# A two-layer hybrid attention encoder: the score products of fourteen head pairs stand one step earlier on TensorE

## The reference, cut to what matters

```python
def mixer_swa_sinks(q, k, v, q_g, k_g, sinks, cos, sin):        # group B; A and C differ in bias, mask and weights
    q = apply_rope(rmsnorm(q, q_g), cos, sin)
    k = apply_rope(rmsnorm(k, k_g), cos, sin)
    ...
    scores = jnp.einsum('bnqhgd,bnjhd->bnhgqj', qc, kb).astype(jnp.float32) * (d ** -0.5)
    ...
    p = jax.nn.softmax(jnp.concatenate([scores, sink], axis=-1), axis=-1)[..., :-1]
    out = jnp.einsum('bnhgqj,bnjhd->bnqhgd', p.astype(v.dtype), vb)

def reference(x, norm1_g, w_in, ...):
    for l in range(DEPTH):                                      # 2
        proj = rmsnorm(x, norm1_g[l]) @ w_in[l]                 # 2048 -> 4352
        ...
        mixed = jnp.concatenate([out_a, out_b, out_c], axis=-1)
        x = x + mixed @ w_out[l]
        h2 = rmsnorm(x, norm2_g[l])
        x = x + jnp.square(jax.nn.relu(h2 @ w_up[l])) @ w_down[l]
```

## Time and profile before

| | |
|---|---|
| median of three runs | 2083.15 us |
| the profiled execution | 2083.34 us |
| its span, first to last instruction | 2081.5 us |
| granted TensorE clock, mean | 1.000 |
| PE busy | 2072.1 us |
| DVE busy | 1270.2 us |
| ACT busy | 993.0 us |
| POOL busy | 190.8 us |

### The profile page before, as it was taken

One profiled execution on the slowest core, in us unless ns is written; L12 is line 12 of the kernel. 1 busy time (PEld: TensorE's weight loads), 2 busy tenths in 40 slices (PEclk: granted clock), 3 DMA queues, 4 the chain that ended last, 5 costly groups with the idle time before them and its releaser, 6 DMA issues.

```text
span 2081.5 us, 26423 instructions
## 1 busy us (share of the span) xinstructions
PE 2072.1 (100%) x10585; PEld 1737.3 (83%) x10585; DVE 1270.2 (61%) x1653; ACT 993.0 (48%) x1328; POOL 190.8 (9%) x196
## 2 busy tenths in 40 slices
PE   8999999999999999999999999999999999999999
PEld 7887788888888888888888877888888888888887
DVE  6767556665565556556676775665655655665664
ACT  5557644443443444344455576444434434443443
POOL 5253100000000000001023521000000000000000
PEclk9999999999999999999999999999999999999999
DMA  8567866666666666666656578666666666666663
GB/s 287 168 189 188 208 197 182 185 192 196 187 191 192 192 187 193 193 187 191 188 176 194 167 192 213 183 185 189 192 193 191 190 194 187 188 193 192 191 191 122
DMA packets 207130, 396.49 MB, mean 190 GB/s; under 512 B 13610, under 2 KB 22032, under 8 KB 207008
## 3 DMA queue, kind: packets, MB, share of 16 engines
q1 hardware_dynamic: 202320, 379.39, 61.5%
q0 software_dynamic: 4512, 15.33, 3.9%
q10 hardware_dynamic: 176, 0.09, 0.0%
HBM read 377.95 MB, written 2.12 MB: 183 GB/s over the span
## 4 chain that ended last, share of the span: by engine, by line
PE 99%; DVE 0%; ACT 0%; DMA 0%; issue 0%; SPq 0%; ACTq 0%; DVEq 0%
PE psum L481 40%; PE psum L501 23%; PE psum L485 20%; PE psum L504 12%; PE psum L511 1%; PE psum L572 1%; PE psum L556 1%; PE psum L599 1%; PE psum L559 1%; DVE probs L1016 0%; PE psum L601 0%; DMA x<-in_x_dram 0%; ACT w_hi L676 0%; PE psum L586 0%; PE psum L587 0%; PE psum L585 0%
## 5 line engine op out<-in xcount | busy, mean ns | idle before, releaser
L852 DVE TENSOR_TENSOR w_lo<-raw_ring,w_hi 128x1024 fp32r<-128x1024 f32 (+1 forms) x692 | 847.1, 1226 | 683.6 <-ACT w_hi L676 682.6
L676 ACT CAST w_hi<-raw_ring 128x1024 fp32r<-128x1024 f32 (+1 forms) x720 | 749.6, 1042 | 1002.0 <-PE psum L485 612.1
L501 PE MATMUL psum<-xt,w_hi 128*128 128x512 f32 x2048 | 512.9, 392 | 0.0
L481 PE MATMUL psum<-w_hi,ht_hi 128*128 128x512 f32 x1280 | 502.1, 392 | 0.0
L481 PE MATMUL psum<-w_hi,ht_lo 128*128 128x512 f32 x1280 | 498.6, 390 | 0.0
L501 PEld LDWEIGHTS psum<-xt,w_hi 128*128 128x128 f32 x2048 | 368.8, 189 | 66.3
L485 PE MATMUL psum<-w_lo,ht_hi 128*128 128x512 f32 x1280 | 342.5, 389 | 0.0
L504 PEld LDWEIGHTS psum<-xt,w_lo 128*128 128x128 f32 x2048 | 279.4, 190 | 20.0
L504 PE MATMUL psum<-xt,w_lo 128*128 128x256 f32 x2048 | 285.6, 282 | 0.0
L481 PE MATMUL psum<-w_hi,xt 128*128 128x512 f32 (+1 forms) x1152 | 282.9, 388 | 1.4 <-DVE xt L889 1.4
L481 PEld LDWEIGHTS psum<-w_hi,ht_hi 128*128 128x128 f32 x1280 | 240.4, 188 | 51.7 <-issue 3.0
(11 more groups left out here) (144 smaller groups left out, 987.0 us busy)
## 6 DMA issues: line engine op xcount, KB each, us to landing
raw_ring<-in_w_up_dram SPq DMA_DIRECT2D x256, 512.0 KB, 3.7
raw_ring<-in_w_down_dram SPq DMA_DIRECT2D x256, 512.0 KB, 3.7
raw_ring<-in_w_in_dram SPq DMA_DIRECT2D x128, 512.0 KB, 4.4
raw_ring<-in_w_out_dram SPq DMA_DIRECT2D x64, 512.0 KB, 4.5
w_lo<-raw_ring POOLq DMA_DIRECT2D x28, 512.0 KB, 5.6
raw_ring<-in_w_in_dram SPq DMA_DIRECT2D x16, 256.0 KB, 2.8
x<-in_x_dram SPq DMA_DIRECT2D x8, 256.0 KB, 7.6
out_dram<-x SPq DMA_DIRECT2D x3, 512.0 KB, 2.7
```

The costliest lines, as they stand in the source:

```text
L481: pe.matmul(bank[r][:, 0:cols], t[:, kt, r * P:(r + 1) * P], w_hi[:, slot, j, 0:cols], start=first and j == 0 and n == 0, stop=False, skip ...
L501: pe.matmul(bank[:, f, :], w_hi[:, w, j, f * P:(f + 1) * P], both, start=kt == 0, stop=False, skip_group_check=True)
L676: act.copy(w_hi[:, u % AHEAD, :, 0:cols], raw_ring[:, u % RAWS, :, 0:cols]).then_inc(hi_ready, 1)
L852: dve.tensor_tensor(w_lo[:, u % AHEAD, :, 0:cols], raw_ring[:, u % RAWS, :, 0:cols], w_hi[:, u % AHEAD, :, 0:cols].bitcast(F32), ALU.subtr ...
```

## The change

PE issues the scores of a pair by a table of its own, `SCORES_AT`: for pairs 0 and 1 the step is the same as in `PAIR_AT`, for pairs 2 to 15 it is one less. In PE's `mix` the scores now come before the transposes of the probabilities, so that the order in a step is V, S, T, Q. The tables of all other engines are unchanged: DVE still masks at the step of `PAIR_AT`.

```diff
+SCORES_AT = {s - (n >= 2): n for s, n in PAIR_AT.items()}
 EXPS = {s + 1: n for s, n in PAIR_AT.items()}
...
                 if s in VALUES:
                     values(pl, s, VALUES[s])
+                if s in SCORES_AT:
+                    scores(pl, SCORES_AT[s])
                 if s in PROBS_T:
                     transpose_probs(pl, PROBS_T[s])
-                if s in PAIR_AT:
-                    scores(pl, PAIR_AT[s])
```

## The result

| | before | after |
|---|---|---|
| median of 22 runs | 2083.12 us (2081.90 to 2084.05) | 2085.85 us (2084.84 to 2086.60) |
| ratio to before | | 1.0013, 95% interval 1.0008 to 1.0019 |
| the profiled execution, and its span | 2083.34, 2081.5 us | 2085.87, 2084.1 us |
| granted TensorE clock, mean | 1.000 | 1.000 |

The change costs 2.7 us, 0.13%. That is within the 0.2% that was called no change, but with 22 runs it is clear of noise, and it is just above the end of the forecast's range (2085.8). The forecast was 2083.4.

What follows compares the result with a forecast made beforehand. PE's own held time was taken to bound the kernel. The terms -1.7 - 0.2 + 0 + 2.2 gave +0.3 us, so 2083.4 us was forecast, with a range of 2081.9 to 2085.8.

Steps and rivals of the forecast that it cites:

- What bounds the kernel: PE's own held time bounds it; an edit counts by distances between PE's group starts or waits put on PE.
- Term 1: Scores behind V of 64 columns, twelve pairs: one change of shape less, -0.14 us each, -1.7 us in all.
- Term 3: Scores of pairs 4, 5, 6, 12, 13, 14, alone or exchanged with a T: as many shape changes, 0.
- Rival B: S behind V saves nothing, since column halves to row halves costs as much as T-S plus S-Q: 2085.1 us, 26%.
- The rule of the drain: Changing tiling mode drains the engine; by it alone twelve pairs save 0.09 each, -1.1 us instead of -1.7.
- Term 2: Scores behind V of C, steps 32 and 36, four in all: one interruption of units less, -0.05 each, -0.2 us.
- Term 4: Start of group B: S waits for DVE's masks, 0.98 and 0.47, less 0.36 of T's old wait; +2.2 us in all.
- Rivals C and D: C: second mask wait absent, 2082.5 us, 9%. D: no mask wait at all, 2080.5 us, 7%.
- Later the margin is enough: After group B's start, S of pair 8 has 1.3 us of cover over the mask of pair 7, so no wait.
- Rival E: Mask late in every even step, DVE's chain from T 1.83 longer: S waits, some 6 us in all, 2089.4 us, 5%.

Runs made afterwards that it cites:

- the kernel with the start kept and the panel copy ahead: Changed kernel, but scores of pairs 4, 5, 6 at their old steps and DVE's panel copy ahead of the weights in steps 57 and 65: 2081.45 us.

## Why the prediction was wrong

**What bounds the kernel**: right. Every difference is in the distance of PE's starts or a wait of PE.

**Term 1, S behind V of 64 columns**: right in mechanism and size. V to S 0.32, S to T 0.43, the even step 4.69 (4.67 forecast), the odd one 3.53 (3.55). The bounds came from -0.24 to +0.14 a pair, and the value taken, from the nearest row, was -0.14; -0.15 is measured. Terms 1 and 2 were to save 0.94 in a layer, and the kernel with the start kept and the panel copy ahead saves 0.92 with a wait of 0.14 in step 58, so 1.06 without it. Term 3 was put at 0; steps 67 to 83 show -0.22, of which pair 15 was to give -0.14, so some -0.08 belongs to it. Rival B is refuted by these savings, though the measured 2085.85 stands near its 2085.1.

**The rule of the drain** (the Trainium skill, TensorEngine Tiling (Array Packing), Tiling Modes) holds in the count: a step pair with one change of tiling mode less is shorter. One drain less at 0.09 was the size that the prediction worked out by that rule alone; the measured saving is 0.15, which is the way in (0.09) and the way out (0.05) of the earlier trace rows together. T between two changes of shape costs 0.15 more than T in its own shape, too (0.48 against 0.33). In the kernel before, the weight load of T behind a unit starts 0.23 ahead of T's matmuls (175.20), and that of S behind T starts only with those of S (175.62):

```profile
174.97 0.48 PEld L572 LDWEIGHTS psum<-const,probs 128*128 128x128 f32 x3
175.62 0.30 PEld L556 LDWEIGHTS psum<-kb_t,qk_t 64*128 64x128 f32 x4 [0.17 <-issue]
```

Whether this is what makes the price was not tested.

**Term 2**: -0.12 in steps 32 to 48 of a layer, -0.10 forecast.

**Term 4, the waits of S**: right. 0.98 and 0.47 forecast, 1.06 and 0.42 measured; steps 48 to 54 are longer by 1.21, of which the forecast has 1.09. The experiment that moves these three pairs alone costs 2.3 us by the medians and 2.1 by its layers, against the 2.2 forecast. Rivals C and D did not occur: the weights took 2.77 again.

**The step that failed** is the sentence "Later the margin is enough". I worked out the cover of one waiter only, the S that was moved. What the shorter odd step brings forward is everything on PE behind it, the V of the next step first, which comes 0.7 before S. V waits for the bank that Q used, and with it for DVE's panel copy. Its cover before was 0.33 in step 58, a fourth of what I found for S. In step 66 it was 0.70 (copy done at 219.45, V at 220.15), from these rows of DVE and PE in the kernel before:

```profile
218.77 0.68 DVE L877 TENSOR_TENSOR panel<-psum,cur 128x512 f32<-128x512 f32 x1
```
```profile
220.15 0.55 PE L599 MATMUL psum<-probs_t,v_b 128*64 128x192 f32 x4
```

Neither cover stands in a row that I had selected. The odd steps 57 and 63 are shorter by 0.91 and 0.94, and V waits 0.76 in step 58 and 0.27 in step 66, 1.16 a layer with their small consequences (steps 58 and 66 are longer than the undisturbed 4.69 and 3.91 by 0.83 and 0.33). Twice 1.16 is 2.3; with it the sum of +0.3 becomes 2.6, which is what the traces show. That it fits to a tenth is partly luck: the waits of S cost 0.12 a layer more than forecast (1.21 for 1.09), and the saving was 0.14 more (1.21 + 1.16 - 1.29 = 1.08 for 0.94). Rival E was near this in kind, a wait in even steps from a chain on DVE that is longer than its cover, but it put the wait before S, and asked for a delay of 1.3 that nothing gave.

The reason given for the cover was that T of the even step ends with its step as before, so that DVE keeps its distance to the next step's start. In step 56 that is nearly so (DVE gets from the copy of T to its next work in 0.65 where it was 0.51, the rest being a wait for ACT), and it is just why V of step 58 waits: the copy keeps its distance, and V comes 0.91 nearer. In step 66 the reason itself is wrong. The odd step 65 before it is 3.54 in both kernels, and in step 64 it is not T that DVE waits for but ACT's copy of the values, 0.79, behind the eviction of chunk 7. ACT comes to this copy 5.1 after its cast at the end of unit 63 in both kernels (208.87 to 213.99 before, 210.92 to 216.05 after), but T of step 64 now comes 0.92 sooner behind that cast, as step 63 has lost its S. The trace of the changed kernel shows this row of DVE in step 64:

```profile
216.47 0.43 DVE L1022 TENSOR_TENSOR ht_lo<-psum,ht_hi 128x256 fp32r<-128x256 f32 x1 [0.79 <-ACT ht_hi L758]
```

Taking that copy forward removed the wait of step 66 whole, and of that of step 58 only 0.17.

## What to carry to other kernels

When work is taken out of a step of the engine that bounds the kernel, everything behind it on that engine arrives earlier. List every waiter in the next steps with the end of what it waits for and its start in the trace before, and not just the moved instruction; the cover is the difference, and a cover below the amount taken out became a wait at both places here (0.33 and 0.70 against 0.91 and 0.94). The thing waited for has waits of its own, and its cover has to be listed too: ACT's copy in step 64 was done 0.07 before DVE needed it (214.39 and 214.46). A wait that is removed ahead of another late event moves there in full (1.06 + 0.42 became 1.56): fix the order at both, or at neither. The change was worth keeping once the other engine's order followed it: the same PE stream with DVE reordered in four steps of a layer went from 2085.9 to 2079.9 us.

## What the runs showed of the hardware that I had not expected

Going from matmuls in 128*64 form to 64*128 form costs PE no more than going from 128*64 to 128*128: 0.32 us from V's second half to the next group in both cases. A group of three transposes between two changes of form holds PE 0.48 us, against 0.33 between groups of its own form and 0.42 ahead of one change.

The weights of pair 4 took 2.77 us for work that takes 0.94 elsewhere, in the same place in the kernels with and without the change, with POOL's rotary products running beside it; whether they are the cause wasn't tried.
